# Feed-forward orders changed in four places, and one weight sum of four per unit made by GpSimd

## The chip, the core and the metric

The kernel runs on one core of a Trainium2 chip. The metric is the device time of one execution in microseconds. A profile comes from one profiled execution. In its views PE is TensorE (matmuls), PEld its weight loads, DVE VectorE, ACT ScalarE, POOL GpSimd, SP SyncE. A name ending in q (SPq, DVEq) is the sequencer of that engine.

## The reference

Two residual blocks run one after the other on x of 256 tokens by 1024, all in fp32. The change touches only the feed-forward part of the first block, which has two layers, and a matrix-vector product of the second block that is computed beside it:

```python
for layer in range(DEPTH):                      # first block, DEPTH = 2
    ...                                         # four mixers, x = x + concat(...) @ w_out
    h = rmsnorm(x, norm_ffn[layer])             # 256 x 1024
    x = x + (jax.nn.silu(h @ w_gate[layer]) * (h @ w_up[layer])) @ w_down[layer]   # D_FF = 2816
...
c_act = jax.nn.silu(c)                          # second block
for i in range(DEPTH):
    mods = (c_act @ ada_w[i] + ada_b[i])        # 1024 x 6144 weights, one row
```

## The kernel before

Every engine has its own program, written out by hand, and waits on counting semaphores. For each layer L the first block runs the input projection, the mixers, the output projection and then the feed-forward stage.

**Units.** The gate and up products are made in N_FU = 8 units k. An even unit is a piece of w_gate, an odd one the same piece (352 columns of each half) of w_up. Each unit is a 2 x 2 block product made with seven products instead of eight (P1 to P7; eight matmuls of 128 x 352 each). For this, four weight sums per unit are needed, each 128 x 1408 in fp32: T1 (L1538), T3 (L1542, in place in the weights), T2 (L1544) and T4 (L1551). P5 uses T1, P6 uses T2, P7 uses T3, P4 uses T4. Four activation sums (S1 to S4) are made once per layer. TensorE's order in a unit is P1(k), P3(k-1), P2(k), P4(k-1), P6(k), then the sums of `ada_sums(k)` (L961), P7(k), P5(k). All products go through `accumulate` (L907).

**Results.** ScalarE copies the running sums P1, P6, P5 of a bank to SBUF (`kept`, L1231); P5 and P3, which add to the same bank, wait for these copies. VectorE combines them with the other products (`c11`, `c22`, `c12`, `c21`, L1647 to L1666). ScalarE applies silu to the four parts of a gate piece (`gated`, L1243), three of them while the odd unit runs. Both work strictly in the order in which the program has them; the counters "summed" and "taken" count along the lists SUMMED and TAKEN.

**Down.** N_DC = 11 steps c follow, each with `down_sums` and `down_act_sums` on VectorE (L1699 to L1715), transposes of the hidden values (L975) and seven products (L990). The last two steps are interleaved. Then VectorE adds the seven results into x (L1742, L1746, L1750), each addition as soon as its product is done.

**The ada product.** c_act @ ada_w is made beside this: VectorE does N_ADA x 8 = 96 terms of 128 x 512 (`ada_term`, L1610 and L1612), eight for each of 12 column blocks k, in one of two accumulators (`ada_acc`, k % 2). ADA_TERMS says how many terms each of the N_STEPS = 19 steps (8 units, 11 down steps) takes. When block k's terms end in step n, TensorE adds its accumulator over the partitions in step n + 1 (ADA_SUMMED, `ada_sums`), and VectorE adds the bias (`ada_row`, L1628) and ScalarE stores the row (`ada_store`, L1214) in step n + 2 (ADA_ROWS). `ada_term(k, 0)` waits on `ada_ps` until the accumulator's last user is summed. In the last step, N_STEPS - 1, `ada_sums(N_STEPS - 1)` stands behind all products in TensorE's program, and `ADA_ROWS[N_STEPS]` stands ahead of the additions into x in VectorE's program and ahead of the copy of the last P1 in ScalarE's. Both lists are empty in this kernel.

**Loads.** SyncE issues `up_load(0)`, `ada(0)`, `ada(1)`, `up_load(1)`, `ada(2)` and then one set per step. `up_load(1)` waits until the output projection is done (`y_ps`). GpSimd rotates some heads at the start of a layer (`rotate_diff`), loads the ada bias (`ada_bias`) and then the small parameters of the next layer (`params`); in the second block it multiplies tap matrices (L1961).

```python
        weight_sum_1(0)
        weight_sums_32(0)
        ...
        mixed(0, 0)          # x += output projection, then the sum of squares
        mixed(0, 1)
        normed(0)
```

Of the kernel before, what the change touches and what calls it, by code (L numbers as in the profile page):

```python
# [86 lines left out]

SUMMED = [("T1", 0), ("T3", 0), ("T2", 0), ("S2", 0), ("S3", 0), ("S4", 0), ("T4", 0)]
for _k in range(N_FU + 1):
    if _k > 0:  # L90
        if _k < N_FU:
            SUMMED.append(("T1", _k))
        SUMMED += [("c22", _k - 1)] + ([("hid22", _k - 1)] if _k % 2 == 0 else [])
        SUMMED += [("T3", _k), ("T2", _k)] if _k < N_FU else [("down", 0)]
        if _k % 2 == 0:
            SUMMED.append(("hid12", _k - 1))
    if _k < N_FU:
        SUMMED += [("c11", _k)] + ([("hid11", _k)] if _k % 2 == 1 else [])
# [7 lines left out]
for _k in range(N_FU):  # L106
    if _k > 0:
        TAKEN.append(("P5", _k - 1))
    TAKEN.append(("P1", _k))
    if _k % 2 == 0:  # L110
        TAKEN.append(("silu11", _k))
    else:
        TAKEN += [("silu22", _k - 1), ("silu12", _k - 1), ("silu21", _k - 1)]
    TAKEN.append(("P6", _k))
TAKEN.append(("P5", N_FU - 1))
TAKEN += [("turned", _c) for _c in range(N_DC)] + [("last", 0)]
# [17 lines left out]

N_ADA = 12
ADA_SLOTS = (0, 1, 5)


N_STEPS = N_FU + N_DC
ADA_TERMS = [6] + [9] * (N_FU - 1) + [3] * 9 + [0] * (N_DC - 9)  # L140
ADA_FIRST = [sum(ADA_TERMS[:n]) for n in range(N_STEPS + 1)]
# [3 lines left out]
def ada_step(k):  # L145
# [9 lines left out]

PER_LAYER = {"xp": 4, "tr": 8, "hT_d": 4, "hT_s": 4, "ssq": 3, "std": 3, "rstd": 1, "z_ps": 12, "z_act": 6, "z_dve": 6, "rope": 3, "rope_b": 1,
             "prep_ps": N_PREP, "prep_ev": N_PREP, "gates_in": 1, "gate_lam_in": 2, "gate_lam_out": 2, "gate_rows": 1, "gate_cols": 1, "conv": 1, "uc": 1,
# [59 lines left out]
def place(nc, m):  # L217
# [82 lines left out]
    m.hidT_a = [at.rearrange("p (k t) -> p k t", k=8) for at in (m.late[:, 0:8 * P], m.hT[:, 0:4, :].rearrange("p j t -> p (j t)"))]  # L300
    m.ada_acc = q[:, 7168:8192].rearrange("p (b n) -> p b n", b=2)
    m.ada_b = q[:, 5632:7168].rearrange("p (k n) -> p k n", k=N_ADA)
# [94 lines left out]
def first_sync(nc, sp, m, a):  # L397

    s = m.s
    for L in range(DEPTH):  # L400
# [107 lines left out]
def first_pool(nc, pool, m, a):  # L508
# [21 lines left out]
    def ada_bias(L):  # L530

        pool.wait_ge(s["rope_b"], nth(L, "rope_b", 1))
        pool.wait_ge(s["o_final"], nth(L, "o_final", 2))
        pool.wait_ge(s["o_done"], nth(L, "o_done", N_UNITS))
        pool.dma_start(m.ada_b[0:P:32], a["ada_b_2"][L].rearrange("(k g n) -> g k n", k=N_ADA, g=4)).then_inc(m.ada_bias, 16)

    def rotate_diff(L):
# [6 lines left out]
        for i in range(TILES):  # L544
            last = rotate(nc.gpsimd, pool, m, m.rz_b, m.tmp_pool, i, [(z_heads(m, i, Z_BQ, 16, 32), 0, 16, 32)])
        last.then_inc(s["rope_b"], 1)

    params(0)
    pool.wait_ge(m.consts_in, 16 * m.n_consts)
    for L in range(DEPTH):  # L550
        rotate_diff(L)
        ada_bias(L)
        if L < DEPTH - 1:
            params(L + 1)
# [51 lines left out]
def first_tensor(nc, pe, m):  # L606
# [5 lines left out]
    for L in range(DEPTH):  # L612
# [297 lines left out]
        def up_product(k, name):  # L910
# [151 lines left out]
def first_scalar(nc, act, m):  # L1062
# [5 lines left out]
    for L in range(DEPTH):  # L1068
# [176 lines left out]
        for k in range(N_FU):  # L1245
# [30 lines left out]
def first_vector(nc, dve, m):  # L1276
# [8 lines left out]
    for L in range(DEPTH):  # L1285
# [385 lines left out]
        for k in range(N_FU):  # L1671
# [1483 lines left out]
```

## Time and profile before

| what | value |
|---|---|
| three runs | 2069.62, 2069.8, 2076.03 us, median 2069.8 |
| profiled execution, its own time | 2073.47 us |
| its span | 2071.7 us, 21123 instructions |
| granted TensorE clock, mean | 0.97 |
| TensorE busy | 92% |
| VectorE busy | 42% |
| GpSimd busy | 4% |
| feed-forward stages | about 190 to 425 us and 604 to 831 us |

A timeline row gives the start in us from the span's start, the duration, the engine, the line of the kernel, what is written and read with the shape, a count, and in brackets how long the engine was idle before it and what released it. The granted clock is given as a share of TensorE's full speed of 2.4 GHz; 0.50 is the level of 1.2 GHz.

### The profile page before, as it was taken

The page shows a single profiled execution, that of the slowest core. Times are in us where ns is not written, and L with a number is a line of the kernel's source. Part 1 is how long each engine was busy: PE and PEld are TensorE (multiplying, and loading weights), DVE is VectorE, ACT ScalarE, POOL GpSimd, SP SyncE. Part 2 cuts the span into 40 slices and gives each one's busy share as a digit, 9 for nine tenths or more (in the row PEclk, how much of TensorE's full clock was granted, in tenths as well). Part 3 has the DMA queues.
Part 4 walks back from the last instruction along what each step waited for, and adds up shares of the span by engine and source line. Part 5 has one row for each costly group of instructions (what it writes and reads, how often), then busy time and mean ns, then how long its engine had stood idle before and what let it go on. Part 6 is the DMA issues. An engine that isn't in the chain of part 4 may idle for free.

```text
span 2071.7 us, 21123 instructions
## 1 busy us (share of the span) xinstructions
PE 1898.6 (92%) x8030; PEld 965.4 (47%) x8030; DVE 863.3 (42%) x1560; ACT 332.1 (16%) x783; POOL 87.1 (4%) x129
## 2 busy tenths in 40 slices
PE   8988999999889999899999999998998999889886
PEld 4555555445555654765434343333775333323321
DVE  1466688834767888765111111112325011111113
ACT  2442111024421111222100010000102000000000
POOL 3102000001020000300000000000000000000000
PEclk9999999999999999999999999999999999999999
DMA  9215767562157677555999999999355999999995
GB/s 309 83 57 163 256 251 279 212 227 62 57 193 288 230 264 264 189 183 191 374 414 428 426 428 428 427 428 407 113 192 214 384 430 428 427 429 427 428 426 232
DMA packets 149241, 603.12 MB, mean 291 GB/s; under 512 B 16584, under 2 KB 60536, under 8 KB 121232
## 3 DMA queue, kind: packets, MB, share of 16 engines
q1 hardware_dynamic: 144064, 591.43, 72.6%
q0 software_dynamic: 4880, 10.22, 1.8%
q8 instruction: 68, 1.11, 0.2%
q14 instruction: 37, 0.30, 0.0%
q10 hardware_dynamic: 192, 0.05, 0.0%
HBM read 597.67 MB, written 1.10 MB: 289 GB/s over the span
## 4 chain that ended last, share of the span: by engine, by line
PE 62%; DMA 24%; DVE 7%; DVEq 2%; issue 2%; ACT 1%; ACTq 1%; SPq 1%
PE ps L2487 14%; DMA ring<-in_e_w_gate 13%; PE ps L907 10%; DMA ring<-in_e_w_up 8%; PE ps L635 7%; PE ps L990 6%; PE ps L2319 4%; PE ps L2505 4%; PE ps L2251 3%; PE ps L2332 3%; PE ps L731 2%; PE ps L2431 2%; PE ps L2416 1%; DMA ring<-in_e_w_down 1%; DMA ring<-in_w_up 1%
## 5 line engine op out<-in xcount | busy, mean ns | idle before, releaser
L2487 PE MATMUL ps<-ring,hT 128*64 128x512 f32 (+1 forms) x1056 | 240.4, 607 | 33.6 <-DMA ring<-in_e_w_up 17.2
L2505 PE MATMUL ps<-ring,qkT 128*64 128x512 f32 (+1 forms) x1024 | 226.6, 594 | 9.9 <-ACT qkT L2707 7.9
L2487 PE MATMUL ps<-ring,late 128*32 128x512 f32 (+1 forms) x928 | 211.1, 609 | 24.0 <-DMA ring<-in_e_w_up 12.7
L635 PE MATMUL ps<-ring,hT 128*128 128x512 f32 (+1 forms) x384 | 169.3, 592 | 3.0 <-DMA ring<-in_w_in 2.2
L2487 PEld LDWEIGHTS ps<-ring,hT 128*64 128x64 f32 (+1 forms) x1056 | 77.3, 126 | 193.1 <-issue 193.1
L2976 DVE TENSOR_TENSOR qkT<-ps,qkT 128x512 f32<-128x512 f32 (+1 forms) x64 | 44.2, 690 | 255.6 <-PE ps L2505 255.6
L2999 DVE TENSOR_TENSOR qkT<-ps,qkT 128x512 f32<-128x512 f32 (+1 forms) x32 | 22.1, 690 | 297.8 <-PE ps L2487 297.8
L2487 PEld LDWEIGHTS ps<-ring,late 128*32 128x32 f32 (+1 forms) x928 | 68.6, 125 | 161.9 <-issue 161.9
L2505 PEld LDWEIGHTS ps<-ring,qkT 128*64 128x64 f32 (+1 forms) x1024 | 70.9, 123 | 146.2 <-issue 146.2
L1612 DVE SCALAR_TENSOR_TENSOR qkT<-ring,cc,qkT 128x512 f32<-128x512 f32 x168 | 125.9, 749 | 8.5
L635 PEld LDWEIGHTS ps<-ring,hT 128*128 128x128 f32 x384 | 72.3, 195 | 80.0 <-issue 70.3
L2995 DVE TENSOR_TENSOR x<-ps,x 128x1024 f32<-128x1024 f32 x22 | 26.9, 1225 | 195.4 <-PE ps L2416 195.4
L907 PE MATMUL ps<-qkT,O 128*128 128x352 f32 x256 | 86.7, 484 | 12.5 <-ACT ring L1231 9.2
L2704 ACT ACTIVATE qkT<-ps 128x512 f32<-128x512 f32 (+1 forms) x32 | 19.0, 594 | 447.5 <-PE ps L2487 447.5
L907 PE MATMUL ps<-ring,hT 128*128 128x352 f32 x256 | 84.3, 473 | 4.9 <-DMA ring<-in_w_up 3.1
L2416 PE MATMUL ps<-qkT 128*128 128x512 f32 x176 | 87.3, 618 | 0.0
L2319 PE MATMUL ps<-hT,ring 128*128 128x256 f32 x384 | 84.8, 384 | 1.5 <-DVE hT L2764 0.9
L990 PE MATMUL ps<-ring,late 128*128 128x512 f32 x168 | 79.8, 600 | 6.5 <-DVE qkT L1628 3.0
L907 PE MATMUL ps<-ring,O 128*128 128x352 f32 x256 | 82.7, 466 | 0.0
L2319 PEld LDWEIGHTS ps<-hT,ring 128*128 128x128 f32 x384 | 73.9, 193 | 12.5 <-DVE hT L2764 1.3
L2431 PE MATMUL ps<-qkT,O 128*128 128x228 f32 (+2 forms) x320 | 70.2, 360 | 1.4 <-DVEq L2957 1.4
L907 PEld LDWEIGHTS ps<-qkT,O 128*128 128x128 f32 x256 | 50.0, 199 | 44.7 <-ACT ring L1231 10.3
(433 smaller groups left out, 2238.8 us busy)
## 6 DMA issues: line engine op xcount, KB each, us to landing
ring<-in_e_w_down SPq DMA_DIRECT2D x64, 2048.0 KB, 17.0
ring<-in_e_w_up SPq DMA_DIRECT2D x64, 2048.0 KB, 17.3
ring<-in_e_w_gate SPq DMA_DIRECT2D x60, 2048.0 KB, 17.5
ring<-in_ada_w SPq DMA_DIRECT2D x24, 2048.0 KB, 14.2
ring<-in_w_gate SPq DMA_DIRECT2D x16, 1408.0 KB, 8.7
ring<-in_w_up SPq DMA_DIRECT2D x16, 1408.0 KB, 9.3
ring<-in_w_down SPq DMA_DIRECT2D x22, 1024.0 KB, 5.1
ring<-in_w_in SPq DMA_DIRECT2D x8, 2048.0 KB, 11.6
```

The source lines that it names most:

```text
L635: last = mm(m.ps[:, 4 + i, 0:chunk_width(n)], m.hT[:, j, i * P:(i + 1) * P], w[:, j, :], start=(j == 0), stop=(j == KC - 1))
L907: last = mm(m.ps[:, bank, 0:FQ], stationary, moving, start=start and j == 0, stop=stop and j == len(left) - 1, skip_group_check=True)
L990: return mm(m.ps[:, bank, :], left, right, start=(c == 0), stop=(c == N_DC - 1))
L1612: last = stt(acc, w, m.cc[:, j:j + 1], acc, ALU.mult, ALU.add)
L2251: last = mm(m.ps[:, c % 4, half * SEQ + lo:half * SEQ + hi], w[half][:, j, at:at + P], m.hT[:, j, lo:hi], start=(j == 0), stop=(j == KC - 1))
L2319: last = mm(dst, w[half][:, j, at:at + P], m.hT[:, j, :], start=(j == 0), stop=(j == KC - 1))
L2332: last = mm(m.ps[:, 4 + 2 * i + n, :], vT[:, j, i * P:(i + 1) * P], w[:, j, :], start=(j == 0), stop=(j == KC - 1))
L2416: last = mm(m.ps[:, 6 + n, :], m.GwT[:, i, :], half_of(m.ye, n), start=True, stop=True)
L2431: last = mm(m.ps[:, k % depth, n * SLOTS:n * SLOTS + width], hN, m.G[l][:, i].rearrange("p x s -> p (x s)")[:, 0:width], start=(i == 0), s ...
L2487: last = mm(dst, xg[:, j, at + x * n_tok:at + x * n_tok + place], w(x, j), start=(j == 0), stop=(j == KC - 1))
L2505: lasts[x] = mm(dst, m.hidT[:, j, rows + x * place:rows + (x + 1) * place], half_of(w(x, j), n), start=(j == 0), stop=(j == 3))
L2976: tt(half_of(m.ye[rows], n), m.ps[rows, 4 + n, :], half_of(m.gf[rows], n), ALU.mult).then_inc(t["ye"], 1)
```

## The change

Five edits are made together.

- ScalarE: in an odd unit the silu of part (1, 0) of the gate piece moves behind the copy of P6.
- SyncE: `up_load(1)` is issued ahead of `ada(1)`.
- Three ada accumulators instead of two. With them the sum of block k waits for `ada_row` k instead of k - 1.
- ADA_TERMS: seven terms instead of nine in unit 7, two instead of three in the first down step, three in the nine steps after it.
- T3 of every unit is made by GpSimd, which waits for T1; P7 waits for it. Its eight instructions per layer stand between `rotate_diff` and `params`, `ada_bias` behind the first of them.

```diff
-SUMMED = [("T1", 0), ("T3", 0), ("T2", 0), ("S2", 0), ("S3", 0), ("S4", 0), ("T4", 0)]
+SUMMED = [("T1", 0), ("T2", 0), ("S2", 0), ("S3", 0), ("S4", 0), ("T4", 0)]
...
-        SUMMED += [("T3", _k), ("T2", _k)] if _k < N_FU else [("down", 0)]
+        SUMMED.append(("T2", _k) if _k < N_FU else ("down", 0))
...
-        TAKEN += [("silu22", _k - 1), ("silu12", _k - 1), ("silu21", _k - 1)]
+        TAKEN += [("silu22", _k - 1), ("silu12", _k - 1)]
     TAKEN.append(("P6", _k))
+    if _k % 2 == 1:
+        TAKEN.append(("silu21", _k - 1))
...
+N_ACC = 3
...
-ADA_TERMS = [6] + [9] * (N_FU - 1) + [3] * 9 + [0] * (N_DC - 9)
+ADA_TERMS = [6] + [9] * 6 + [7] + [2] + [3] * 9 + [0] * (N_DC - 10)
...
-    m.ada_acc = q[:, 7168:8192].rearrange("p (b n) -> p b n", b=2)
+    m.ada_acc = q[:, 7168:8704].rearrange("p (b n) -> p b n", b=N_ACC)
...
         up_load(0)
         ada(0)
+        up_load(1)
         ada(1)
-        up_load(1)
         ada(2)
...
+    def weight_sum_3(L, k):
+
+        pool.wait_ge(s["summed"], after(L, "summed", "T1", k))
+        b12, b22 = [m.up_raw[k % 2][1][:, h * QUARTER:(h + 1) * QUARTER] for h in range(2)]
+        nc.gpsimd.tensor_tensor(b12, b22, b12, ALU.subtract).then_inc(s["pool_out"], 1)
...
     for L in range(DEPTH):
         rotate_diff(L)
-        ada_bias(L)
+        for k in range(N_FU):
+            weight_sum_3(L, k)
+            if k == 0:
+                ada_bias(L)
...
             elif name == "P7":
                 summed("S3", 0)
+                ready("pool_out", 1 + k + 1)
...
                 if n < N_FU:
-                    if L > 0 or k >= 2:
-                        ready("ada_row", k - 1)
+                    if L > 0 or k >= 1:
+                        ready("ada_row", k)
                     dst = m.ps[:, 6, k % 2 * P:(k % 2 + 1) * P]
...
-                    last = mm(dst[32 * g:32 * (g + 1), :], m.ones[:, 0:32], m.ada_acc[:, k % 2, g * P:(g + 1) * P], start=True, stop=True)
+                    last = mm(dst[32 * g:32 * (g + 1), :], m.ones[:, 0:32], m.ada_acc[:, k % N_ACC, g * P:(g + 1) * P], start=True, stop=True)
...
                 gated(k - 1, 0, 1)
+            kept(k, "P6")
+            if k % 2 == 1:
                 gated(k - 1, 1, 0)
-            kept(k, "P6")
...
-        def weight_sums_32(k):
-
-            tt(quarter(k, 0, 1), quarter(k, 1, 1), quarter(k, 0, 1), ALU.subtract).then_inc(s["summed"], 1)
+        def weight_sum_2(k):
+
             dve.drain()
             tt(m.up_sum[1], quarter(k, 1, 1), m.up_sum[0], ALU.subtract).then_inc(s["summed"], 1)
...
-                if L > 0 or k >= 2:
-                    dve.wait_ge(s["ada_ps"], nth(L, "ada_ps", k - 1))
+                if L > 0 or k >= N_ACC:
+                    dve.wait_ge(s["ada_ps"], nth(L, "ada_ps", k - N_ACC + 1))
...
-            acc = m.ada_acc[:, k % 2, :]
+            acc = m.ada_acc[:, k % N_ACC, :]
```

## Rows read from the trace of the kernel before

**Rows 1.** Page, part 1: engine, busy us, share of the span, instructions.

```profile
PE 1898.6 (92%) x8030; PEld 965.4 (47%) x8030; DVE 863.3 (42%) x1560; ACT 332.1 (16%) x783; POOL 87.1 (4%) x129
```

**Rows 2.** Timeline, TensorE, layer 0: start, duration, instructions, [idle before and releaser].

```profile
209.24 5.06 PE L907 MATMUL ps<-ring,hT 128*128 128x352 f32 x8 [3.06 <-DMA ring<-in_w_up]
...
216.98 2.53 PE L907 MATMUL ps<-ring,hT 128*128 128x352 f32 x8
219.34 2.53 PE L907 MATMUL ps<-qkT,hT 128*128 128x352 f32 x8
```

**Rows 3.** Stretches of time, layer 0: busy per engine, granted clock, DMA share, GB/s.

```profile
209.00:211.00 2.00, 1.76 (x3) 1.17 (x4) 1.78 (x2) 0.00 (x0) 0.00 (x0) 0.50 0.62 239
```

**Rows 4.** Timeline, SyncE's queue, layer 0.

```profile
189.25 8.13 SPq L451 DMA_DIRECT2D ring<-in_w_up  x2
```

**Rows 5.** Page, part 6: DMA issues, KB each, median us to landing.

```profile
ring<-in_w_up SPq DMA_DIRECT2D x16, 1408.0 KB, 9.3
```

**Rows 6.** Timeline, TensorE, layer 1, unit 3.

```profile
664.05 2.61 PE L907 MATMUL ps<-qkT,O 128*128 128x352 f32 x8 [0.66 <-DVE qkT L1544]
...
674.38 5.06 PE L907 MATMUL ps<-qkT,O 128*128 128x352 f32 x8 [4.58 <-ACT ring L1231]
```

**Rows 7.** Timeline, VectorE, layer 1, units 2 and 3.

```profile
636.18 1.63 DVE L1538 TENSOR_TENSOR qkT<-ring 128x1408 f32<-128x1408 f32 x1 [0.94 <-PE ps L907]
...
648.40 0.49 DVE L1610 TENSOR_SCALAR qkT<-ring,cc 128x512 f32<-128x512 f32 x1 [5.63 <-PE ps L961]
...
658.65 1.61 DVE L1538 TENSOR_TENSOR qkT<-ring 128x1408 f32<-128x1408 f32 x1
...
662.33 1.63 DVE L1544 TENSOR_TENSOR qkT<-ring,qkT 128x1408 f32<-128x1408 f32 x1
667.16 0.49 DVE L1610 TENSOR_SCALAR qkT<-ring,cc 128x512 f32<-128x512 f32 x1 [3.20 <-PE ps L961]
...
677.38 0.49 DVE L1628 TENSOR_TENSOR qkT<-ps,qkT 128x128 f32<-128x128 f32 x2
```

**Rows 8.** Timeline, VectorE, layer 1, start of the stage.

```profile
596.82 0.68 DVE L1560 TENSOR_TENSOR x<-ps,x 128x512 f32<-128x512 f32 x1
...
600.42 0.17 DVE L1570 RECIPROCAL small<-small 128x1 f32<-128x1 f32 x1 [0.63 <-ACT small L1207]
```

**Rows 9.** Groups by form, GpSimd: count, busy us, mean ns.

```profile
L499 POOL TENSOR_TENSOR qkT<-qkT 128x512 f32<-128x512 f32 x4 | 5.1, 1266 | 4.7 <-issue 4.4
...
L1961 POOL TENSOR_TENSOR qkT<-fold,z 128x1024 f32<-128x1024 f32 x1 | 1.9, 1905 | 0.0
```

**Rows 10.** Timeline, VectorE, beside a GpSimd instruction.

```profile
830.61 0.15 DVE L383 TENSOR_TENSOR small<-small 128x1 f32<-128x1 f32 x1
...
832.80 1.87 DVE L383 TENSOR_TENSOR small<-small 128x1 f32<-128x1 f32 x1
```

**Rows 11.** Timeline, GpSimd, the same stretch.

```profile
832.43 2.22 POOL L1961 TENSOR_TENSOR z<-fold,z 128x1024 f32<-128x1024 f32 x1 [2.28 <-PE ps L2351]
```

**Rows 12.** Timeline, VectorE, last additions of layer 0, then of layer 1.

```profile
415.19 0.28 DVE L1628 TENSOR_TENSOR qkT<-ps,qkT 128x128 f32<-128x128 f32 x1
416.67 0.69 DVE L1746 TENSOR_TENSOR qkT<-ps,qkT 128x512 f32<-128x512 f32 x1 [1.19 <-ACT qkT L1271]
...
422.50 1.29 DVE L1742 TENSOR_TENSOR x<-ps,x 128x512 f32<-128x512 f32 x2 [0.45 <-PE ps L990]
424.28 0.69 DVE L1742 TENSOR_TENSOR x<-ps,x 128x512 f32<-128x512 f32 x1 [0.49 <-PE ps L990]
...
824.11 0.69 DVE L1746 TENSOR_TENSOR qkT<-ps,qkT 128x512 f32<-128x512 f32 x1 [1.19 <-ACT qkT L1271]
...
830.85 0.69 DVE L1742 TENSOR_TENSOR x<-ps,x 128x512 f32<-128x512 f32 x1
```

**Rows 13.** Timeline, TensorE, last products of layer 0, then of layer 1.

```profile
423.15 1.02 PE L990 MATMUL ps<-ring,late 128*128 128x512 f32 x2
...
829.47 1.02 PE L990 MATMUL ps<-ring,late 128*128 128x512 f32 x2
```

More of the change, by code:

```diff
@@ L154 @@
 N_UNITS = len(UNITS)
-PER_LAYER = {"xp": 4, "tr": 8, "hT_d": 4, "hT_s": 4, "ssq": 3, "std": 3, "rstd": 1, "z_ps": 12, "z_act": 6, "z_dve": 6, "rope": 3, "rope_b": 1,
+PER_LAYER = {"xp": 4, "tr": 8, "hT_d": 4, "hT_s": 4, "ssq": 3, "std": 3, "rstd": 1, "z_ps": 12, "z_act": 6, "z_dve": 6, "rope": 3, "pool_out": 1 + N_FU,
              "prep_ps": N_PREP, "prep_ev": N_PREP, "gates_in": 1, "gate_lam_in": 2, "gate_lam_out": 2, "gate_rows": 1, "gate_cols": 1, "conv": 1, "uc": 1,
@@ L530, in ada_bias @@
     def ada_bias(L):
-        pool.wait_ge(s["rope_b"], nth(L, "rope_b", 1))
+        pool.wait_ge(s["pool_out"], nth(L, "pool_out", 1))
         pool.wait_ge(s["o_final"], nth(L, "o_final", 2))
@@ L545, in rotate_diff @@
             last = rotate(nc.gpsimd, pool, m, m.rz_b, m.tmp_pool, i, [(z_heads(m, i, Z_BQ, 16, 32), 0, 16, 32)])
-        last.then_inc(s["rope_b"], 1)
+        last.then_inc(s["pool_out"], 1)
+    def weight_sum_3(L, k):
+        pool.wait_ge(s["summed"], after(L, "summed", "T1", k))
+        b12, b22 = [m.up_raw[k % 2][1][:, h * QUARTER:(h + 1) * QUARTER] for h in range(2)]
+        nc.gpsimd.tensor_tensor(b12, b22, b12, ALU.subtract).then_inc(s["pool_out"], 1)
     params(0)
@@ L791, in diff_batch @@
         def diff_batch():
-            pe.wait_ge(s["rope_b"], nth(L, "rope_b", 1))
+            pe.wait_ge(s["pool_out"], nth(L, "pool_out", 1))
             pairs(batch(B_DIFF), [cols(m.rz_b, k * P) for k in range(4)]).then_inc(s["prep_ps"], 1)
@@ L1553, in first_vector @@
         weight_sum_1(0)
-        weight_sums_32(0)
+        weight_sum_2(0)
         def mixed(i, c):
@@ L1677, in first_vector @@
                 c22(k - 1)
-                weight_sums_32(k)
+                weight_sum_2(k)
                 ada_terms(at, at + 2)
```

## The prediction

> **What bounds the kernel now.** I read the page first. TensorE is busy for 92% of the span [rows 1], so a change in VectorE's work is worth only what it does to TensorE's pauses. The change touches the feed-forward stage of both layers (about 190 to 425 and 604 to 831 us), so I went through TensorE's timeline there. Its normal pace is one product (eight matmuls) per 2.37 us (216.98 to 219.34 in [rows 2]), hence 7 x 2.37 + 0.4 for the sums on ones = 17.0 to 17.1 us per unit. Three kinds of pause stand out.
>
> First, in layer 0, P1 of unit 1 waits 3.06 us for the w_up piece. The next two products then take 216.98 - 209.24 = 7.74 us instead of 2 x 2.37: another 3.0 us [rows 2], because the granted clock is 0.50, the 1.2 GHz level, after the pause [rows 3]. So this pause costs 6.1 us. SyncE issues the w_up piece at 189.25, behind two ada_w loads of 2 MB, and its issue alone takes 8.13 us [rows 4]. In layer 1 the same spot has no pause.
>
> Second, in unit 3 of both layers (here layer 1): P6 waits 0.66 us for T2, P5 waits 4.58 us for ScalarE's copy (L1231), and the slow clock shows in the 5.06 us of that block [rows 6]; 0.66 + 4.58 + 3.05 = 8.3 us per layer. ScalarE is late because `silu21` stands before the copy and needs `c21`, which is late because VectorE waited 5.63 and 3.20 us for `ada_ps` [rows 7], two accumulators being too few.
>
> Third, the last additions. VectorE makes `ada_row(11)` at 415.19, and all additions into x from 416.67 on overlap TensorE's last products; they end at 424.97, 0.8 us after TensorE's last product (423.15 + 1.02 = 424.17) [rows 12, 13]. In layer 1: 831.54 against 830.49.
>
> **The up piece.** With `up_load(1)` ahead of `ada(1)` one ada_w load instead of two lies before it. It is issued at the same 189.25 (it waits for `y_ps`), and a w_up load lands 9.3 us after its issue in the median [rows 5], so at about 199 to 201, and TensorE asks at 206.2. What moves behind it, `ada(1)` and `ada(2)` (2 MB each), is asked for by VectorE a unit or two later. GpSimd's 17 small parameter loads for layer 1 also leave this stretch: they now stand behind the eight weight sums, at about 330 us, beside the first two w_down loads (1 MB each, issued at P3 of unit 6 and used five products or 12 us later). Gain: 6.1 us, layer 0 alone; nothing if the load is still late.
>
> **The weight sum on GpSimd.** VectorE loses T3, 1.6 us as T2 in [rows 7] and 1.7 with its drain. GpSimd's time for 128x1408 is not in the trace. Its nearest rows: 1266 ns for 128x512 in place, 1905 ns for 128x1024 [rows 9]; scaled by length these give 3.5 and 2.6 us. I take 3.0, between them, since T3 has two streamed inputs and is in place like the first. P7 asks for T3 over 10 us after T1, so TensorE doesn't wait for it.
>
> What VectorE does meanwhile is the question. A VectorE addition of two SBUF columns, 128x1, takes 0.15 us at 830.61 but 1.87 us at 832.80; it ends at 834.67, and GpSimd's TENSOR_TENSOR that began at 832.43 ends at 834.65 [rows 10, 11]. So VectorE instructions with two SBUF inputs stand still while GpSimd works. The Trainium skill says the same (SBUF — State Buffer, section "SBUF: two separate sides"): the shared port pair is an exclusive lock, held for the full instruction, against VectorE instructions with two SBUF inputs. By that rule, the trace agrees; without it the sum would be that of the first rival below.
>
> GpSimd starts as T1 ends. VectorE has c22 (one input from PSUM, not held) and then the second half of c22 or T2, which have two SBUF inputs: held until about T1's start + 1.62 + 0.15 + 3.0 = 4.8 us. Before, T2 began 662.33 - 658.65 = 3.7 us after T1's start [rows 7]. So VectorE ends each unit 1.1 us later than before, not 1.7 earlier (0.6 to 1.6 later, for 2.5 and 3.5 us on GpSimd).
>
> **The start of the stage.** T1(0), T2(0), T3(0) run just before `mixed`, which began at 596.82 with no gap [rows 8]: VectorE is on the path there. T3 on GpSimd now runs beside T2 and the sum of squares, which both read SBUF twice. If GpSimd gets the ports first, T2 is held until 4.8 us after T1's start, where all three sums ended before, and `mixed` is 1.5 us later; if VectorE does, GpSimd runs from 3.3 to 6.3 and holds the sum of squares, due at 5.6, for 0.7 us. 0.3 us of either is covered by ScalarE's table load (VectorE waited 0.63 us at 600.42). I take 0.8 us per layer, bounds 0 and 1.7.
>
> **Unit 3 after the change.** Three accumulators remove the 5.63 and 3.20 us waits, and the copy of P6 no longer stands behind `silu21`. But the diff also makes the sum for k = 2 wait for `ada_row` k instead of k - 1. Both k = 1 and k = 2 are summed in unit 3 of TensorE, while `ada_row(1)` stands at the start of VectorE's unit 4 (ADA_ROWS). So TensorE now stops between P6 and P7 of unit 3 until VectorE has done all of unit 3. In layer 1: VectorE's work from T1 of unit 2 to the rows took 677.38 - 636.18 = 41.2 us, less 5.63 + 3.20 of waits = 32.4 [rows 7]; plus 2 x 1.1 = 34.6, so `ada_row(1)` ends at 636.18 + 34.6 + 0.3 = 671.1. TensorE, with no wait before P6 (663.4), is there at 666.1. It stands 5.0 us, and after such a pause the clock falls as before: 5.0 + 3.05 = 8.1, against 8.3 lost now. The stall changes its name and is worth 0.2 us per layer.
>
> **Units 4 to 7.** The 32.4 us are 16.2 per unit, 17.3 with the hold, against TensorE's 17.1, and an even unit (with `c12` and a longer c22) is some 1 us longer than an odd one; so VectorE falls behind by 1 to 2 us until unit 7, whose seven terms give it back. Its cover: P6 starts 4 x 2.37 = 9.5 us after P1, and T2 ended 0.3 + 3.7 + 1.6 = 5.6 us after it; less 1.1 and the lag, nearly 1 us is left. So nothing at 3.0 us on GpSimd, and about 2 us per layer at 3.5.
>
> **Terms.** ADA_TERMS now ends one step later: the last term is in step 17, so the sum for k = 11 falls in step 18 (`ada_sums(N_STEPS - 1)`), which stands behind TensorE's very last product, and `ada_row(11)` and its store fall in ADA_ROWS[N_STEPS], which stand before VectorE's additions into x and before ScalarE's copy of the last P1. What overlapped is now in series. Layer 0: TensorE ends at 424.17, the sum 0.4, row at 424.7; from row to first addition 1.48 us as now (store, copy), so 426.2; the additions took 424.97 - 416.67 = 8.3 us, less waits 0.45 and 0.49 = 7.4 [rows 12]; end at 433.6 instead of 424.97: 8.6 us. Layer 1: 830.49 + 0.5 + 1.5 + 7.43 = 839.9 instead of 831.54: 8.4 us. Nothing hides them: the next stage begins with transposes of x. In addition TensorE stands about 7 us, so its clock falls: up to 3 us each time by [rows 2]; I take 2.5 in layer 0 and, as an estimate that no row here carries, 0.7 in layer 1, where short pieces of work follow whose pauses let the clock fall already.
>
> **Sum.** -6.1 (up piece) + 1.6 (start) - 0.4 (unit 3) + 17.0 (last additions) + 3.2 (clock) = +15.3 us. The profiled execution took 2073.5 us (span 2071.7), 3.7 above the median of 2069.8; this difference belongs to no part of the change, so the sum is put on the median: **2085 us**. Its own range: start 0 to 3.4, clock 0 to 6, GpSimd's length -2 to +4: 2078 to 2093.
>
> **Rivals.**
> *GpSimd doesn't hold VectorE* (or hardly): VectorE gains 1.7 us per unit. T1 of unit 3 is then bound by P5 of unit 2 (636.2 + 17.1 = 653.3), unit 3 takes 677.38 - 658.65 - 3.20 - 1.7 = 13.8, with the row it ends at 667.4, TensorE stands 1.3 us with no fall of the clock, and the start costs nothing. 2085 - 2 x 6.8 - 1.6 = 2070: not slower. It decides where VectorE finishes unit 3 within about 2.5 us after TensorE's first sum. Against it: [rows 10, 11]. 0.13.
> *The last additions are hidden* by something behind them: 2085 - 20 = 2065, 0.04; and together with the first rival 2050 or less, which is faster, 0.08. Against both: no wait on a load at layer 1's first products.
> *GpSimd takes 3.5 us or more*: VectorE's lag reaches TensorE in units 6 and 7: 2090, 0.12. Here the rule that speaks against the edit bears: the Trainium skill (GPSIMD Engine Reference, section "Performance versus the Vector engine") gives 4497 ns for 2048 columns, an estimate of 3.1 us for 1408, by which the sum stays as it is.
> *The change doesn't do what it says in layer 0*: the w_up piece still lands late: 2091, 0.05.
> My forecast: 0.58.
>
> **Numbers.** A measurement of this kernel can tell about 0.3% (6 us). Slower: 0.58 + 0.12 + 0.05 = 0.75. Same: 0.13 + 0.04 = 0.17. Faster: 0.08. The range takes in the first rival, my own range and the slower cases: 2067 to 2095; outside are the hidden additions and the ends.
>
> **What would show it.** Right: TensorE's wait at 209.24 gone; in unit 3 a wait of about 5 us before a sum on ones (L961's place) released by `ada_row`, none before P5; GpSimd TENSOR_TENSOR 128x1408 at 3 us with VectorE instructions behind it of 3 us or more; `ada_row` as the first VectorE instruction after TensorE's last product, and TensorE idle about 7 us before the next stage. Wrong: additions into x that still begin before TensorE's last products end, or T2 at 1.62 us beside a running GpSimd instruction.

## The result, and the profile after

| | before | after |
|---|---|---|
| median of the runs shown | 2071.89 us (4 runs) | 2087.95 us (4 runs) |
| profiled execution, its own time | 2073.47 us | 2087.13 us |
| its span | 2071.7 us | 2085.2 us |

The changed kernel is slower: ratio 1.0079, 95% interval 1.0062 to 1.0096, or 16 us on the medians and 13.5 us on the spans. The forecast was 2085 us, 15.3 us more than before.

In the changed kernel the lines are numbered anew: L919 is a product of the up blocks, L974 a sum on ones, L1003 a down product, L365 the transposes of x, L647 the input projection of the next layer; on VectorE L1552 is T1, L1557 T2, L1641 `ada_row`, L1755, L1759 and L1763 the last additions; L555 is T3 on GpSimd. Page, part 1, busy time of each engine (before: [rows 1]):

```profile
PE 1898.9 (91%) x8030; PEld 965.3 (46%) x8030; DVE 878.5 (42%) x1544; ACT 334.4 (16%) x783; POOL 136.3 (7%) x145
```

TensorE does the same work. VectorE has 16 instructions fewer and is busy 15 us longer: it got slower, not lighter. Timeline of TensorE, feed-forward stages (start, duration, line, count, in brackets the idle time before and what ended it):

```profile
192.97 2.63 PE L919 MATMUL ps<-ring,hT 128*128 128x352 f32 x8 [1.36 <-DVE hT L372]
...
208.00 2.53 PE L919 MATMUL ps<-ring,hT 128*128 128x352 f32 x8
...
259.72 0.65 PE L974 MATMUL ps<-qkT,ones 128*32 128x128 f32 x8 [5.69 <-DVE qkT L1641]
260.31 4.26 PE L919 MATMUL ps<-ring,O 128*128 128x352 f32 x8
...
679.21 0.65 PE L974 MATMUL ps<-qkT,ones 128*32 128x128 f32 x8 [5.85 <-DVE qkT L1641]
```

P1 of unit 1 (208.00) no longer waits for its weights, where [rows 2] had 3.06 us. P5 of unit 3 no longer waits for ScalarE, as in [rows 6]; in both layers a sum on ones waits instead, for the row that VectorE makes late. Timelines of VectorE and GpSimd, start of the stage and unit 1:

```profile
179.49 1.62 DVE L1552 TENSOR_TENSOR qkT<-ring 128x1408 f32<-128x1408 f32 x1
181.20 4.62 DVE L1557 TENSOR_TENSOR qkT<-ring,qkT 128x1408 f32<-128x1408 f32 x1
...
208.27 1.63 DVE L1552 TENSOR_TENSOR qkT<-ring 128x1408 f32<-128x1408 f32 x1 [0.54 <-PE ps L919]
...
210.42 4.21 DVE L1557 TENSOR_TENSOR qkT<-ring,qkT 128x1408 f32<-128x1408 f32 x1
```
```profile
181.19 3.15 POOL L555 TENSOR_TENSOR ring<-ring 128x1408 f32<-128x1408 f32 x1 [95.09 <-DVE qkT L1552]
...
209.99 3.16 POOL L555 TENSOR_TENSOR ring<-ring 128x1408 f32<-128x1408 f32 x1 [25.04 <-DVE qkT L1552]
```

T2 takes 4.62 us in unit 0 and 4.21 in unit 1 instead of 1.63 [rows 7], and 4.2 in the other odd units; in the even ones behind unit 0 the held instruction is the second half of c22 (3.09 us instead of 0.52, at 227.10). T2 is held until GpSimd's sum is over, and then takes its own time: 209.99 + 3.16 + 1.6 = 214.75 against the measured end at 214.63. Last additions of layer 0, TensorE and then VectorE, and TensorE in layer 1:

```profile
417.12 1.02 PE L1003 MATMUL ps<-ring,late 128*128 128x512 f32 x2
418.07 0.43 PE L974 MATMUL ps<-qkT,ones 128*32 128x128 f32 x8
425.58 1.94 PE L365 MATMUL ps<-ident,x 128*128 128x128 f32 x8 [7.08 <-DVE x L1755]
428.08 1.94 PE L365 MATMUL ps<-ident,x 128*128 128x128 f32 x8 [0.55 <-DVE hT L372]
430.78 22.58 PE L647 MATMUL ps<-ring,hT 128*128 128x512 f32 x48 [0.76 <-DVE hT L372]
...
846.94 1.04 PE L2364 MATMUL ps<-ident,late 39*128 39x39 f32 x8 [9.13 <-DVE x L1755]
```
```profile
418.57 0.29 DVE L1641 TENSOR_TENSOR qkT<-ps,qkT 128x128 f32<-128x128 f32 x1 [7.01 <-PE ps L974]
420.05 0.69 DVE L1759 TENSOR_TENSOR qkT<-ps,qkT 128x512 f32<-128x512 f32 x1 [1.19 <-ACT qkT L1285]
```

In [rows 12, 13] the additions began at 416.67 and TensorE's last product at 423.15. Now the order is last product, sum, row, store, additions, next stage, in series: TensorE stands 7.08 and 9.13 us. The stretches of time behind the pause of layer 0 (busy us and count of each engine, then granted clock, DMA share, GB/s) show the clock at its lower level:

```profile
424.00:428.00 4.00, 1.94 (x8) 1.57 (x8) 3.85 (x10) 1.06 (x4) 0.00 (x0) 0.50 1.05 386
428.00:432.00 4.00, 3.16 (x10) 2.30 (x11) 2.81 (x8) 2.69 (x8) 0.00 (x0) 0.50 1.08 362
432.00:436.00 4.00, 4.00 (x7) 1.54 (x7) 0.17 (x1) 0.09 (x1) 0.00 (x0) 0.71 1.10 355
```

Cut at fixed instructions, the two profiled executions differ as follows. "Start" goes from T1(0) to P1(0), "up" from P1(0) to the first down product, "down" from there to the first product of the next stage (L647 in layer 0; in layer 1 the long run of conformer products, L2264 at 860.76).

| stretch | before | after | difference |
|---|---|---|---|
| start, layer 0 / layer 1 | 12.30 / 12.30 | 13.48 / 13.47 | +1.2 / +1.2 |
| up, layer 0 / layer 1 | 151.47 / 144.83 | 143.66 / 143.99 | -7.8 / -0.8 |
| down, layer 0 / layer 1 | 85.40 / 97.66 | 94.15 / 104.47 | +8.8 / +6.8 |
| 48 products L647 behind it, layer 0 | 20.84 | 22.58 | +1.7 |
| mixers of layer 1, eight products L647 | 3.60 | 5.29 | +1.7 |

Their sum is +12.8 us; another 0.8 us had already gone by before the first stage, at T1(0) (178.71 and 179.49), where the change has done nothing yet. In the other kernels of this document T1(0) starts between 178.42 and 181.10, so this much is scatter.

### The profile page after: what moved, and what is told of

It reads as the page before. It is cut to its first block, busy times and chain, and to the rows that moved or that the text cites. A ratio compares the mean times of both kernels' runs of the same rounds, so it can differ in the third digit from the quotient of the medians.

```text
span 2085.2 us, 21127 instructions
## 1 busy us (share of the span) xinstructions
PE 1898.9 (91%) x8030; PEld 965.3 (46%) x8030; DVE 878.5 (42%) x1544; ACT 334.4 (16%) x783; POOL 136.3 (7%) x145
## 4 chain that ended last, share of the span: by engine, by line
PE 64%; DMA 21%; DVE 8%; DVEq 2%; issue 2%; ACT 2%; ACTq 1%; SPq 1%
PE ps L2500 15%; DMA ring<-in_e_w_gate 12%; PE ps L919 10%; DMA ring<-in_e_w_up 7%; PE ps L647 7%; PE ps L1003 6%; PE ps L2518 4%; PE ps L2332 4%; PE ps L2264 3%; PE ps L2345 3%; PE ps L2444 2%; PE ps L2429 2%; PE ps L743 1%; DMA ring<-in_e_w_down 1%; PE ps L727 1%
## 5 line engine op out<-in xcount | busy, mean ns | idle before, releaser
L2500 PE MATMUL ps<-ring,hT 128*64 128x512 f32 (+1 forms) x1056 | 245.4, 618 | 33.7 <-DMA ring<-in_e_w_gate 19.2
L2500 PE MATMUL ps<-ring,late 128*32 128x512 f32 (+1 forms) x928 | 206.1, 597 | 23.0 <-DMA ring<-in_e_w_up 13.3
L647 PE MATMUL ps<-ring,hT 128*128 128x512 f32 (+1 forms) x384 | 173.7, 605 | 2.7 <-DMA ring<-in_w_in 1.9
L647 PEld LDWEIGHTS ps<-ring,hT 128*128 128x128 f32 x384 | 74.0, 199 | 82.6 <-issue 72.7
L2332 PE MATMUL ps<-hT,ring 128*128 128x256 f32 x384 | 85.3, 385 | 1.5 <-DVE hT L2777 0.9
L1003 PE MATMUL ps<-ring,late 128*128 128x512 f32 x168 | 80.4, 601 | 7.0 <-DVE qkT L1641 3.0
L919 PE MATMUL ps<-ring,O 128*128 128x352 f32 x256 | 85.6, 479 | 0.0
L919 PE MATMUL ps<-ring,hT 128*128 128x352 f32 x256 | 81.2, 460 | 2.7 <-DVE hT L372 2.7
L919 PE MATMUL ps<-qkT,O 128*128 128x352 f32 x256 | 81.3, 460 | 1.8 <-ACT qkT L1244 1.5
L555 POOL TENSOR_TENSOR ring<-ring 128x1408 f32<-128x1408 f32 x16 | 50.6, 3162 | 429.4 <-DVE qkT L1552 429.4
```

What stands on the lines that cost most here:

```text
L555: nc.gpsimd.tensor_tensor(b12, b22, b12, ALU.subtract).then_inc(s["pool_out"], 1)
L647: last = mm(m.ps[:, 4 + i, 0:chunk_width(n)], m.hT[:, j, i * P:(i + 1) * P], w[:, j, :], start=(j == 0), stop=(j == KC - 1))
L919: last = mm(m.ps[:, bank, 0:FQ], stationary, moving, start=start and j == 0, stop=stop and j == len(left) - 1, skip_group_check=True)
L1003: return mm(m.ps[:, bank, :], left, right, start=(c == 0), stop=(c == N_DC - 1))
L2332: last = mm(dst, w[half][:, j, at:at + P], m.hT[:, j, :], start=(j == 0), stop=(j == KC - 1))
L2500: last = mm(dst, xg[:, j, at + x * n_tok:at + x * n_tok + place], w(x, j), start=(j == 0), stop=(j == KC - 1))
```

## The experiments

All times in the table are medians, the ratios are against the kernel before, run on the same chip in the same batch. Start, up and down are the stretches above in layer 0, up 1 in layer 1.

| kernel | us | ratio (95% interval) | start | up | up 1 | down |
|---|---|---|---|---|---|---|
| before | 2069 to 2072 | 1 | 12.3 | 151.5 | 144.8 | 85.4 |
| changed | 2087.95 | 1.0079 (1.0062, 1.0096) | 13.5 | 143.7 | 144.0 | 94.2 |
| k1_terms | 2071.76 | 1.0005 (0.9993, 1.0018) | 13.5 | 143.7 | 143.8 | 86.1 |
| k2_banks | 2073.83 | 1.0015 (1.0003, 1.0027) | 13.5 | 136.0 | 136.1 | 94.3 |
| k3_vec | 2080.85 | 1.0056 (1.0038, 1.0073) | 12.3 | 141.8 | 142.3 | 93.8 |
| k5_terms_banks | 2058.10 | 0.9940 (0.9924, 0.9956) | 13.5 | 136.0 | 136.0 | 88.9 |
| k6_all_vec | 2051.37 | 0.9908 (0.9886, 0.9930) | 12.3 | 135.9 | 135.9 | 85.3 |
| k4_up | 2066.96 | 0.9985 (0.9972, 0.9998) | 12.3 | 145.2 | 143.9 | 85.5 |
| k8_t3_alone | 2073.47 | 1.0017 (1.0004, 1.0029) | 13.5 | 145.8 | 147.2 | 85.0 |
| k9_up_silu | 2061.02 | 0.9956 (0.9939, 0.9973) | 12.3 | 139.8 | 139.9 | 85.4 |
| k11_params | 2067.86 | 0.9987 (0.9977, 0.9997) | 12.3 | 145.0 | 143.9 | 85.4 |

**k1_terms: the changed kernel with the old term counts.**

```diff
-ADA_TERMS = [6] + [9] * 6 + [7] + [2] + [3] * 9 + [0] * (N_DC - 10)
+ADA_TERMS = [6] + [9] * (N_FU - 1) + [3] * 9 + [0] * (N_DC - 9)
```

> The changed kernel with the term counts of before put back (the last three columns of the ada rows end three down blocks earlier); all else stays changed. My theory, that the last row and the last additions stand in series behind the last down product because of the new counts: the pauses of 7.08 us (layer 0) and 9.13 us (layer 1) before TensorE's next work go back to about 0 to 2 us, the first z products run at full clock again, and the time falls by 8.9 + 1.7 + 7.0 = about 17 us against the changed kernel, to about 2070 us. Rival, that the tail is late for another reason (GpSimd's hold on VectorE, the three accumulators): the pauses stay and the time moves by under 3 us. The pause in unit 3 should stay (5.7 and 5.9 us) in both.

Measured: 2071.76 us, 16 us less than the changed kernel. TensorE's timeline at the transposes of x in layer 0 and at the first work of the conformer in layer 1:

```profile
420.50 2.40 PE L365 MATMUL ps<-ident,x 128*128 128x128 f32 x16 [0.49 <-issue]
...
832.37 0.66 PE L2364 MATMUL ps<-ident,late 39*128 39x39 f32 x8 [0.94 <-DVE x L1755]
```

The pauses of 7.08 and 9.13 us are gone, the granted clock is 1.00 from 424 to 436 us, and unit 3 keeps its 5.69 and 5.85 us. The loss at the end of the layers comes from two terms moved from the up blocks into a tenth down step. What is left of it in layer 0, 86.1 against 85.4 us, is a longer wait at the first down step, shown with k6 below.

**k2_banks: the sums on ones in two PSUM banks in turn, waiting one row further back.**

```diff
-                    if L > 0 or k >= 1:
-                        ready("ada_row", k)
-                    dst = m.ps[:, 6, k % 2 * P:(k % 2 + 1) * P]
+                    if L > 0 or k >= 2:
+                        ready("ada_row", k - 1)
+                    dst = m.ps[:, 6 + k % 2, 0:P]
```

`ada_row` reads from the same place, and the first hidden transposes wait for the last of these rows. The sum of k + 1 now never writes the bank from which row k is still being read. The wait and the bank are changed together; the wait alone was not tried.

> The changed kernel, but the sums on ones go in turn to two PSUM banks and wait for the row one further back, as before the change. Theory, that the pause of 5.7 us in unit 3 of each layer comes from TensorE waiting for the row that VectorE makes late: that pause goes, with the 1.8 us that the lower clock costs behind it; VectorE is behind by some of this, so at least 3.5 us and at most 7.5 us a layer, 7 to 15 us in all against the changed kernel. Rival, that the pause only absorbs a delay that VectorE has anyway and TensorE then waits for VectorE at another line of units 3 and 4: under 2 us a layer. The tail's pauses (7.08 and 9.13 us) stay in both.

Measured: 2073.83 us, 14.1 us less than the changed kernel; the up stretch falls by 143.66 - 135.97 = 7.7 us in layer 0 and by 7.9 in layer 1. No pause of 0.4 us or more is left in units 2 to 7, so the pause did not turn up elsewhere. Of the 7.7 and 7.9 us, 5.69 and 5.85 are the pause; the other 2.0 us are the clock behind it.

**k5_terms_banks: both together.**

> The changed kernel with both: the term counts of before, and two PSUM banks for the sums on ones with the wait one row further back. T3 stays on GpSimd. Theory: the two effects add, about 17 us for the tail and 7 to 15 us for unit 3, so 2049 to 2064 us. Rival, that they share one cause or that one delay turns up again at the other's place: not below 2065 us.

Measured: 2058.10 us. By the ratios, k1 gives 15.3 us, k2 13.2 us, both together 28.8 us (2070 us times the differences of the ratios). The two effects add; no shared cause shows.

**k3_vec: the changed kernel with T3 back on VectorE.**

```diff
     def weight_sum_2(k):
 
+            tt(quarter(k, 0, 1), quarter(k, 1, 1), quarter(k, 0, 1), ALU.subtract).then_inc(s["summed"], 1)
             dve.drain()
```

> The changed kernel with the weight sum T3 back on VectorE; the orders, terms and accumulators stay changed. Theory, that GpSimd's sum holds VectorE for its own 3.16 us and spares it 1.6 us: the start of the stage is 1.2 us shorter in each layer, the pause of 5.7 us in unit 3 is shorter by 2 to 3.5 us in each layer, and the whole is 5 to 9 us below the changed kernel. Rival, that VectorE is truly relieved by 1.6 us a unit: the pause in unit 3 grows by 1.6 to 5 us a layer and the kernel is 3 to 10 us slower than the changed one. The tail's pauses stay.

Measured: 2080.85 us, 7.1 us less by the medians, 4.8 by the ratios. The start has its 12.3 us again. But the pause in unit 3 shrinks only to 4.15 us (4.59 in layer 1), 1.5 and 1.3 us less instead of 2 to 3.5:

```profile
256.19 0.66 PE L964 MATMUL ps<-qkT,ones 128*32 128x128 f32 x8 [4.15 <-DVE qkT L1632]
```

So the larger part of this pause is the wait for row k itself, which stands a full step behind, and not GpSimd.

**k6_all_vec: k5 with T3 on VectorE.**

> The changed kernel with the term counts of before, two PSUM banks for the sums on ones, and T3 back on VectorE. What is left of the change is the up piece, the third accumulator and the silu order. Theory, that GpSimd's sum only costs: the start of the stage is 1.2 us a layer shorter than in the same kernel with T3 on GpSimd, and the time is 2 to 5 us below that one, 2047 to 2062 us. Rival, that VectorE is relieved where TensorE no longer waits for the row: same time or up to 5 us slower than with T3 on GpSimd.

Measured: 2051.37 us, 0.9908 of before: the fastest kernel here, 36.6 us under the changed one. Against k5 it gains 6.7 us, more than the 2 to 5 expected. The start gives 1.2 us a layer; the rest is a pause in the down steps that I had not foreseen. TensorE in k5 and then in k6, second down product of layer 0:

```profile
336.27 1.58 PE L1005 MATMUL ps<-ring,late 128*128 128x512 f32 x2 [2.74 <-DVE late L1730]
```
```profile
333.25 1.13 PE L995 MATMUL ps<-ring,late 128*128 128x512 f32 x2 [0.93 <-DVE late L1721]
```

Where TensorE no longer stops in unit 3, VectorE's lag, which only the kernel with the holds has (the terms are the same in both), comes out at the first down step: 2.74 us, and 3.19 us in layer 1, instead of 0.93. The pause in unit 3 was one cover of this lag and the seven terms in unit 7 the other: with the pause alone (k1) the wait is 1.61 and 2.07 us, with the seven terms alone (k2) 1.09 and 1.54, with both (the changed kernel) 0.93.

**k4_up: before, with the second up load ahead of the second ada column.**

```diff
         up_load(0)
         ada(0)
+        up_load(1)
         ada(1)
-        up_load(1)
```

> The kernel before with one edit: the second up load is queued ahead of the second ada column. Theory: the gap of TensorE at the product of unit 1 in layer 0 goes and the time falls by 6.1 us (5 to 7.5). Rival, that the ada column, now later, holds VectorE instead: 0 to 3 us.

Measured: the gap is gone and the up stretch is 151.47 - 145.22 = 6.25 us shorter, as expected. The medians give only 3.1 us (0.4 to 5.8), less than the 5 to 7.5 expected and close to the upper end of the rival's 0 to 3. The rival's hold of VectorE doesn't show: the up stretch gained all that the gap had cost. The profiled execution of before lies 2 to 4 us above its medians, which is the size of what is missing; whether its other executions have the whole gap isn't shown.

**k8_t3_alone: before, with T3 on GpSimd and nothing else.**

> The kernel before with one edit: T3 is made by GpSimd; all orders, terms and accumulators are those of before. Theory, that GpSimd's sum holds VectorE for about 3.1 us and spares it 1.6: 1.2 us more at the start of each layer, and some of the rest is taken up by VectorE's own waits in units 2 and 3 (5.63 and 3.20 us): 2 to 5 us slower than before. Rival, that there is no hold: 0 to 5 us faster.

Measured: 1.0017 of before, 3.5 us slower. Yet the trace shows something that I had not expected at all: the gap at P1 of unit 1 is gone here too (204.69, 207.16 and 209.53 are blocks without a gap), although `up_load(1)` still stands behind `ada(1)`. The stretches of time of before, and then of this kernel (the last number is GB/s, the one before it the DMA engines' busy share):

```profile
188.00:192.00 4.00, 3.09 (x15) 1.80 (x14) 3.77 (x10) 1.14 (x4) 2.38 (x4) 1.00 0.93 179
192.00:196.00 4.00, 3.41 (x17) 2.27 (x16) 2.86 (x8) 1.37 (x6) 0.00 (x0) 1.00 1.04 278
```
```profile
188.00:192.00 4.00, 2.25 (x11) 1.04 (x9) 3.57 (x9) 1.35 (x5) 0.00 (x0) 1.00 1.01 330
192.00:196.00 4.00, 3.27 (x14) 2.08 (x15) 2.92 (x7) 0.29 (x1) 0.00 (x0) 1.00 1.06 396
```

The DMA engines are busy in both, but before they move 179 and 278 GB/s, here 330 and 396. What left this stretch are GpSimd's 17 small parameter loads, which now stand behind the eight sums. That led to the next run.

**k11_params: before, with these small loads alone moved.**

```diff
         if L < DEPTH - 1:
+            pool.wait_ge(s["summed"], after(L, "summed", "T1", 7))
             params(L + 1)
```

> The kernel before with one edit on GpSimd: its 17 small parameter loads for layer 1 wait until VectorE has made T1 of unit 7, so they leave the start of the up blocks in layer 0; the order of the up and ada loads stays that of before. Theory, that these small loads are what slows the transfers there (179 to 278 GB/s from 184 to 196 us in before, 330 to 396 in the kernel with T3 alone on GpSimd): SyncE's issue of the second up load takes about 1.3 us instead of 8.13, the gap of 3.06 us in layer 0 goes and the time falls by about 6 us (3 to 7). Rival, that it is the second ada column ahead of the up load that makes it late: gap and time stay.

Measured: 0.9987, or 2.7 us less (0.6 to 4.8) where about 6 were expected, as in k4; the up stretch 144.98 us, 6.5 us shorter. SyncE's queue and the same stretch of time as above:

```profile
190.70 1.47 SPq L451 DMA_DIRECT2D ring<-in_w_up  x2
```
```profile
188.00:192.00 4.00, 3.54 (x15) 1.82 (x13) 3.25 (x8) 1.37 (x6) 0.00 (x0) 1.00 1.04 384
```

The issue takes 1.47 us instead of 8.13 [rows 4], at 384 GB/s. So the piece was late only with both, the small loads beside it and two ada loads ahead of it; each of the two edits alone removes the whole gap. In k4 the small loads are still there, and the piece, with one load less ahead of it, comes in time. The same stretch in k4 and then in the changed kernel; the piece is issued at 191.36 and 190.03, so little of it moves here in either:

```profile
188.00:192.00 4.00, 4.00 (x16) 2.08 (x14) 3.18 (x8) 1.37 (x3) 4.00 (x7) 1.00 0.94 51
```
```profile
188.00:192.00 4.00, 3.10 (x13) 1.43 (x11) 3.45 (x8) 1.08 (x5) 0.00 (x0) 1.00 0.15 13
```

With the small loads the DMA engines are busy for 0.94 of it and move 51 GB/s, without them for 0.15.

By k11 and k8, which differ in T3 alone, T3 on GpSimd costs (1.0017 - 0.9987) x 2070 = 6.2 us; k6 against k5 gives 6.6 us and k3 against the changed kernel 4.8 us by their ratios.

**k9_up_silu: before, with the up load and the silu order alone.**

```diff
-        TAKEN += [("silu22", _k - 1), ("silu12", _k - 1), ("silu21", _k - 1)]
+        TAKEN += [("silu22", _k - 1), ("silu12", _k - 1)]
     TAKEN.append(("P6", _k))
+    if _k % 2 == 1:
+        TAKEN.append(("silu21", _k - 1))
```

The order of the instructions in ScalarE's program changes with it, and the up load moves as in k4.

> The kernel before with two edits and no more: the second up load is queued ahead of the second ada column, and in odd units the copy P6 is made ahead of the silu of the second half. T3 is on VectorE, two accumulators, one bank, the term counts of before. Theory, that these two edits are the whole gain of the changed kernel and the third accumulator with its nearer wait only costs: the pauses of 3.06 us (layer 0) and 4.58 us (both layers) go, the up part is 136 us long in both layers as in the kernel with two banks, and the time is 2048 to 2056 us. Rival, that without the third accumulator VectorE or TensorE waits for the other in units 3 to 5: a pause of 1 to 5 us a layer stays and the time is 2057 to 2066 us.

Measured: 2061.02 us, 0.9956: the theory falls, the rival holds. The 4.58 us for ScalarE are gone, but the up stretch is 139.8 us and not 136. With two accumulators VectorE still waits for the sums in units 2 and 3, and TensorE later for VectorE. VectorE, then TensorE, layer 0:

```profile
236.49 0.49 DVE L1613 TENSOR_SCALAR qkT<-ring,cc 128x512 f32<-128x512 f32 x1 [5.63 <-PE ps L963]
...
255.22 0.49 DVE L1613 TENSOR_SCALAR qkT<-ring,cc 128x512 f32<-128x512 f32 x1 [3.20 <-PE ps L963]
```
```profile
271.80 2.60 PE L909 MATMUL ps<-qkT,O 128*128 128x352 f32 x8 [1.15 <-DVE qkT L1547]
```

The third accumulator, with the second bank beside it, is worth about 4 us a layer (k6, 135.9 us), provided its wait isn't moved nearer: k3, with the nearer wait and T3 on VectorE like k6, has 141.8.

**k7_memset and k10_copy: what holds VectorE.** In both GpSimd does something cheaper in T3's place, and T3 is left out.

```diff
-        nc.gpsimd.tensor_tensor(b12, b22, b12, ALU.subtract).then_inc(s["pool_out"], 1)
+        nc.gpsimd.memset(b12, 0.0).then_inc(s["pool_out"], 1)
```

> The changed kernel, but GpSimd writes zeros over the same 128 x 1408 elements where it made T3 (so T3 is left out), in the same place and with the same waits. Theory A, that it is GpSimd's use of SBUF at all that holds VectorE: T2 in odd units still takes the memset's time and more (over 2.5 us instead of 1.62). Theory B, that only an operation that reads SBUF on GpSimd holds VectorE: T2 takes 1.6 us, and the pause in unit 3 shrinks by 2 to 4 us a layer.

In k10_copy the new line is `nc.gpsimd.tensor_copy(b12, b22)`.

> The changed kernel, but GpSimd copies the quarter of 128 x 1408 elements that T3 read first over the one it wrote (so T3 is left out): one operand read and one written, at the same place with the same waits. Theory A, that any GpSimd operation that reads SBUF holds VectorE: T2 takes over 2.5 us in odd units and the start of the stage keeps its 1.2 us. Theory B, that only one with two operands does: T2 takes 1.62 us everywhere, as with the zeros, and the pause in unit 3 is 4.15 us.

Their total times, 2559 and 3030 us, say nothing: with other values the second block reads 799 and 1000 MB instead of 598. Up to 845 us they can be compared. GpSimd, then VectorE's T2, in k7 and then in k10:

```profile
182.78 1.28 POOL L555 MEMSET ring<- 128x1408 f32 x1 [97.45 <-DVE qkT L1552]
```
```profile
182.81 1.62 DVE L1557 TENSOR_TENSOR qkT<-ring,qkT 128x1408 f32<-128x1408 f32 x1
```
```profile
207.71 1.36 POOL L555 COPY ring<-ring 128x1408 f32<-128x1408 f32 x1 [25.64 <-DVE qkT L1552]
```
```profile
208.17 2.38 DVE L1557 TENSOR_TENSOR qkT<-ring,qkT 128x1408 f32<-128x1408 f32 x1
```

Beside the zeros, which only write, T2 takes 1.62 us in all 16 units: theory B of the first. Beside the copy it takes 2.38 us; held until 207.71 + 1.36 = 209.07 it would end at 210.7, and it ends at 210.55. So one operand read is enough for a hold, for as long as the copy runs; the figures of theory A (over 2.5 us in odd units, a longer start) did not come: T2 takes 2.37 or 2.38 us in all odd units, 2.81 in unit 0, and the start is 12.3 us, since the copy is short and T3 is left out. Neither theory's numbers fit as written, the mechanism is that of A. The Trainium skill (SBUF — State Buffer, section "SBUF: two separate sides") has VectorE's instructions with two SBUF inputs locked out only against a GpSimd operation that reads SBUF; these two runs agree.

Both kernels keep a pause of 4.15 us in unit 3 of layer 0, just as k3 does, and although k7's VectorE has neither T3 nor a hold. Its timeline shows why; VectorE had to wait for TensorE's own product:

```profile
249.47 0.52 DVE L1662 TENSOR_TENSOR qkT<-ps,qkT 128x352 f32<-128x352 f32 x1 [2.10 <-PE ps L919]
```

A freer VectorE can't make the row earlier than this: the 4.15 us are the price of waiting for row k.

## Why the prediction was right, and where it wasn't

The forecast of 2085 us is 3 us under the measured median, and its mechanisms were those that the runs showed. Term by term:

- **The up piece**, -6.1: measured -6.25 in k4. The size is right, and the new order is enough, but the cause was only half told. I had put the lateness down to the order, two ada loads ahead. k8 and k11 leave that order and lose the gap as well. My own text named the 17 small loads that leave this stretch and gave them no price; they were the other half. The 8.13 us of [rows 4] alone don't tell: in the changed kernel the issue of the two ada loads takes 6.60 us at 191.33 with no small load beside it, at 375 and 397 GB/s.
- **The weight sum on GpSimd**: 3.0 us taken, 3.16 measured. T2 ends 214.63 - 208.27 = 6.4 us after T1's start, as my 4.8 + 1.6 says. The hold of [rows 10, 11] is confirmed by k3 and k6, in which T2 takes 1.62 us again, and by k7.
- **The start**, 0.8 a layer: 1.2 measured. I averaged over who gets the ports first. GpSimd did, in both layers (181.19 against 181.20), which was the dearer case.
- **Unit 3**: 5.0 + 3.05 = 8.1 us forecast, 7.7 and 7.9 measured by k2. The pause was longer, 5.69 and 5.85, the clock's part smaller, 2.0 us; the 3.05 us that I read into [rows 6] for it was 2.5 (674.38 to 681.65 for two products, less 2 x 2.37). What before lost there was sized too low: the up stretch of layer 1 is 144.83 - 135.91 = 8.9 us over k6, not 8.3. But this differs from one execution to the next: k4 and k11 change nothing in layer 1 and have 143.9 us there, 1 us less than before and as much as the changed kernel. So the 0.8 us that layer 1 gains in the table can't be put down to the change.
- **Units 4 to 7**, nothing: true of the changed kernel. The seven terms of unit 7, which I named, were one half of the cover (k1 against the changed kernel); the other, the time that the pause in unit 3 gives VectorE, I hadn't seen. Without both the lag costs 2.74 and 3.19 us at the first down step (k5).
- **Terms**, 8.6 + 8.4 and 2.5 + 0.7 for the clock: in layer 0 the down stretch grew by 8.8 us and the 48 products by 1.7 more, 10.5 against 11.1. In layer 1 it grew by 6.8 us against 9.1, and most of this difference lies in the kernel before: k4 and k11, whose last steps are those of before, take 96.3 us there where the profiled execution of before took 97.66, so the growth is 8.2 us against them. One thing in it is the small addition of [rows 10], held by GpSimd for 1.87 us. In the changed kernel it takes 0.15 us at 848.05, as GpSimd's multiplication starts at 848.06. In k4 it takes 0.15 us too (829.54), although it starts 0.36 us behind the recorded start of the multiplication (829.18), where in before it was held 0.37 us behind it. So which of the two is held there is a close race, and [rows 10] shows one outcome of it.
- **Not the change's**: 1.7 us in the mixers of layer 1 and 0.8 us ahead of the first stage. The mixers lose the same 1.7 us in k4 and k11, which touch nothing there, and none in k8 and k9 (last section).

Sum: the terms -6.1 + 1.6 - 0.4 + 17.0 + 3.2 = 15.3 stand against -7.8 - 0.8 + 2.4 + 15.6 + 1.7 + 1.7 + 0.8 = 13.6 us of the spans. The 2.3 us too much in layer 1's end and the 1.5 too little in layer 0's up stretch (-7.8 against -6.1 - 0.2) are the largest misses. They and the 2.5 us that aren't the change's partly cancel, so the total is better than its parts, and that it came so close is partly luck. Of the 3 us between forecast and median, 2.1 are the base: before had a median of 2071.9 us beside the changed kernel and 2069.8 when I added up.

The rivals: that GpSimd doesn't hold VectorE falls by the rows above. k7, in which it doesn't, also shows that this rival was priced wrongly: the pause would have been 4.15 us and not 1.3. That the last additions are hidden falls by k1. That VectorE's lag reaches TensorE is real, but one step later than I put it and only once the pause in unit 3 is gone.

## What to carry to other kernels

Read for each moved wait whether it now names something that the other engine makes only a step later: one nearer wait ate more than a third accumulator had won, and putting the wait back, with a second PSUM bank, regained it. A list of work that ends one step later may put two chains in series that overlapped; look at what the last step's instructions stand in front of. And before work goes to GpSimd, ask which VectorE instructions run beside it and whether they read SBUF twice: here each 1.6 us taken off VectorE made another of its instructions 2.6 to 3.0 us longer.

## What the runs showed of the hardware

**Small loads take the DMA engines' time and move little.** With 17 small parameter loads in the stretch the engines are 0.93 and 0.94 busy at 179 and 51 GB/s (before and k4, 188 to 192 us); without them 1.04 busy at 384 (k11). Where k11 has put these loads, the picture comes back:

```profile
324.00:328.00 4.00, 4.00 (x15) 2.63 (x14) 3.53 (x6) 0.34 (x1) 4.00 (x7) 1.00 0.83 80
```

The Trainium skill (DMA: Bandwidth & Descriptors, section "Why small descriptors are slow (HBM only)") puts a fixed overhead on every packet. These rows agree in direction only; its example, 27% for a descriptor of 256 bytes, is far less than what was lost here, and no run shows what made up the rest.

**The clock's price behind a pause varies.** After a pause of 5.69 us in unit 3 the first block took 4.26 us and the clock was back soon:

```profile
261.00:263.00 2.00, 2.00 (x5) 1.20 (x4) 0.00 (x0) 0.00 (x0) 0.00 (x0) 0.50 0.64 231
263.00:265.00 2.00, 2.00 (x8) 1.22 (x7) 0.00 (x0) 0.00 (x0) 0.00 (x0) 0.84 0.02 7
```

This cost 2.0 us. The shorter pauses of 3.06 us [rows 2] and of 4.58 us (layer 0 of before) cost 3.0, that of 4.58 us in [rows 6] 2.5, and the same pause in layer 1 of k4 only 1.6:

```profile
672.06 4.14 PE L907 MATMUL ps<-qkT,O 128*128 128x352 f32 x8 [4.58 <-ACT ring L1231]
676.04 2.53 PE L907 MATMUL ps<-ring,hT 128*128 128x352 f32 x8
```

The mixers of layer 1 lost 1.7 us behind a pause of 1.84 us that cost nothing before:

```profile
546.41 0.66 PE L712 MATMUL ps<-ident,ring 128*128 128x128 f32 x4 [1.84 <-DVE O L1456]
546.90 5.29 PE L647 MATMUL ps<-ring,hT 128*128 128x512 f32 x8
...
548.00:550.00 2.00, 2.00 (x3) 0.71 (x3) 1.93 (x4) 1.51 (x8) 0.00 (x0) 0.50 0.00 0
```

The same eight products, after the same 1.84 us, took 3.60 us in the kernel before, in k8 and in k9, and 5.29 us in k4 and here, in k11:

```profile
537.20 5.29 PE L636 MATMUL ps<-ring,hT 128*128 128x512 f32 x8
```

None of these edits touches the mixers. What decides it was not tried here; a sum of this kind carries 1 to 2 us for each such pause that it can't settle.
